# Two moves in a written-out schedule of a two-block transformer kernel: the order in which VectorE and TensorE handle the state outputs, and where ScalarE takes the squares of the final norm

## What is computed

```python
def ssd_chunked(x, dt, A, Bm, Cm):          # run forward and on the flipped sequence
    ...
    y_diag = jnp.einsum('bcgrls,bcsgrp->bclgrp', Wd, xdt)
    decay_states = jnp.exp(a_cs[..., -1:] - a_cs)
    states = jnp.einsum('bcsgn,bcgrs,bcsgrp->bcgrpn', Bc, decay_states, xdt)
    ...
    _, prev = lax.scan(step, init, (jnp.moveaxis(states, 1, 0), jnp.moveaxis(chunk_decay, 1, 0)))
    prev = jnp.moveaxis(prev, 0, 1)
    y_off = jnp.einsum('bclgn,bcgrpn,bcgrl->bclgrp', Cc, prev, jnp.exp(a_cs))
    return (y_diag + y_off).reshape(b, l, H, P)

        x = x + jnp.square(jax.nn.relu(h @ w_up[i])) @ w_down[i]
    return rmsnorm(x, norm_final)            # x * rsqrt(mean(x*x) + EPS) * g
```

## Time and profile before

| | |
|---|---|
| median of 3 runs | 1835.4 us (1835.2 to 1836.85) |
| the profiled execution, its own time | 1837.07 us |
| its span, first to last instruction | 1835.2 us |
| TensorE clock granted in it | 0.999 |
| TensorE busy | 1792.7 us, 98% |
| VectorE busy | 1178.2 us, 64% |
| ScalarE busy | 847.1 us, 46% |
| GpSimd busy | 260.2 us, 14% |
| chain that ended last | PE 70%, DVE 21%, ACT 5%, issue 4% |

### The profile page before, as it was taken

The page is one execution under the profiler, slowest core; times in us unless marked ns, Lnnn a source line. Parts: engine busy times, 40 slices in busy tenths (PEclk is TensorE's granted clock), DMA queues, the critical chain, the costliest instruction groups (busy, mean ns, idle before and its releaser), DMA issues.

```text
span 1835.2 us, 24785 instructions
## 1 busy us (share of the span) xinstructions
PE 1792.7 (98%) x9602; PEld 1453.2 (79%) x9602; DVE 1178.2 (64%) x1912; ACT 847.1 (46%) x1623; POOL 260.2 (14%) x324
## 2 busy tenths in 40 slices
PE   7999999999999989999999999999999999999997
PEld 7767898888888877878878786767788998888886
DVE  6356544233345788897888955677556358685957
ACT  5255533222224565564655644554434445343434
POOL 0502000000000035254352540000020000000000
PEclk9999999999999999999999999999999999999999
DMA  7211343332322453353443444233544241404211
GB/s 242 81 58 45 98 127 99 108 92 92 92 92 74 150 141 128 117 146 103 151 137 116 138 149 154 88 104 116 138 149 137 68 153 58 161 23 161 76 73 46
DMA packets 128244, 205.69 MB, mean 112 GB/s; under 512 B 26480, under 2 KB 58416, under 8 KB 127488
## 3 DMA queue, kind: packets, MB, share of 16 engines
q1 hardware_dynamic: 118944, 166.83, 28.6%
q0 software_dynamic: 8464, 34.93, 5.5%
q10 hardware_dynamic: 720, 2.36, 0.3%
HBM read 191.37 MB, written 12.71 MB: 111 GB/s over the span
## 4 chain that ended last, share of the span: by engine, by line
PE 70%; DVE 21%; ACT 5%; issue 4%; DMA 0%; POOL 0%; DVEq 0%; ACTq 0%
PE m L2135 13%; PE m L2137 13%; PE m L2136 13%; PE m L2146 5%; PE m L2148 5%; PE m L2147 5%; DVE lo L1387 4%; PE s L2298 3%; DVE X L1791 3%; PE m L2270 2%; PE m L2272 1%; PE m L2271 1%; PE m L2243 1%; PE m L2244 1%; PE m L2245 1%
## 5 line engine op out<-in xcount | busy, mean ns | idle before, releaser
L2135 PE MATMUL m<-hH,hi 128*128 128x512 f32 (+1 forms) x1392 | 531.6, 382 | 2.9 <-DVE hL L1417 1.6
L2137 PE MATMUL m<-hH,lo 128*128 128x512 f32 (+1 forms) x1392 | 509.6, 366 | 0.0
L2136 PE MATMUL m<-hL,hi 128*128 128x512 f32 (+1 forms) x1392 | 509.2, 366 | 0.0
L1387 DVE TENSOR_TENSOR lo<-raw,hi 128x1024 fp32r<-128x1024 f32 x267 | 333.0, 1258 | 162.1 <-ACT hi L913 161.8
L913 ACT ACTIVATE hi<-raw 128x1024 fp32r<-128x1024 f32 x267 | 276.5, 1050 | 176.2 <-PE m L2137 41.8
L2135 PEld LDWEIGHTS m<-hH,hi 128*128 128x128 f32 x1392 | 263.3, 189 | 50.1 <-issue 5.4
L2137 PEld LDWEIGHTS m<-hH,lo 128*128 128x128 f32 x1392 | 263.1, 189 | 43.3
L2136 PEld LDWEIGHTS m<-hL,hi 128*128 128x128 f32 x1392 | 263.6, 189 | 40.0 <-issue 1.0
L2146 PE MATMUL m<-hi,hH 128*128 128x512 f32 (+1 forms) x320 | 134.8, 421 | 1.8 <-DVE lo L1387 1.8
L2148 PE MATMUL m<-hi,hL 128*128 128x512 f32 (+1 forms) x320 | 122.1, 381 | 0.0
L2147 PE MATMUL m<-lo,hH 128*128 128x512 f32 (+1 forms) x320 | 122.0, 381 | 0.0
(11 more groups left out here) (331 smaller groups left out, 3006.9 us busy)
## 6 DMA issues: line engine op xcount, KB each, us to landing
raw<-in_w_in_dram SPq DMA_DIRECT2D x72, 512.0 KB, 3.7
hn<-scr_cs_dram POOLq DMA_DIRECT2D x32, 512.0 KB, 4.2
raw<-in_w_up_dram SPq DMA_DIRECT2D x32, 512.0 KB, 4.9
wq<-in_w_down_dram SPq DMA_DIRECT2D x24, 512.0 KB, 8.4
raw<-in_w_gate_dram SPq DMA_DIRECT2D x44, 256.0 KB, 2.9
raw<-in_w_up_dram SPq DMA_DIRECT2D x44, 256.0 KB, 3.2
raw<-in_w_down_dram SPq DMA_DIRECT2D x22, 512.0 KB, 4.0
raw<-in_w_in_dram SPq DMA_DIRECT2D x33, 256.0 KB, 3.3
```

What stands on the lines that cost most here:

```text
L1387: e.tensor_tensor(d, r, h.bitcast(F32), ALU.subtract).then_inc(s_lo, 1)
L2135: e.matmul(bank, wh[:, kk, c], h[:, k, q], start=k == 0, stop=False)
L2136: e.matmul(bank, wh[:, kk, c], l[:, k, q], start=False, stop=False)
L2137: x = e.matmul(bank, wl[:, kk, c], h[:, k, q], start=False, stop=k == kt - 1)
```

## The change

There are three edits. The third to sixth outputs of the first group of each round go one slot later (slots 33 to 36 become 34 to 37). The squares of results 2, 3, 8 and 9 in `fs3` come at the end of the slot behind the one in which they stood, behind `round_hidden` and `split_weights`. The root's preparation goes from slot 3 of `fs3` to slot 19.

```diff
-ROOT_AT = (s0("wo0") + 2, s0("dn20") + 2, s0("wa0") + 1, s0("fs3") + 3)
+ROOT_AT = (s0("wo0") + 2, s0("dn20") + 2, s0("wa0") + 1, s0("fs3") + 19)
...
-OF_T = [x + s + k for x in X0 for s in (31, 49) for k in range(6)]
+OF_T = [x + s for x in X0 for s in (31, 32, 34, 35, 36, 37, 49, 50, 51, 52, 53, 54)]
...
                 for b, i in DONE_AT.get(g, ()):
-                    final_squares(b, i)
+                    if i >= 10:
+                        final_squares(b, i)
                 round_hidden(g)
                 for j in CONV_AT.get(g, ()):
                     split_weights(j)
+
+                for b, i in DONE_AT.get(g - 1, ()):
+                    if i < 10:
+                        final_squares(b, i)
```

## The result

The changed kernel took 1840.18 us (median of 14 runs, 1838.39 to 1842.75); the kernel before, run between them on the same chip, took 1836.06 us (14 runs, 1835.12 to 1837.25). The ratio is 1.0022, with a 95% interval of 1.0015 to 1.0029: 0.22% slower, where the forecast said no difference, and 2.2 us above the upper end of its range. The runs of a kernel fall in two groups some 1.6 us apart (before: seven of 1835.12 to 1835.45 and seven of 1836.67 to 1837.25), and one execution of the kernel before in a later set, 3822.78 us, enters no comparison. Three of the 14 runs of the changed kernel are in its lower group (1838.39 to 1838.61), so the medians are 4.1 us apart and the lower groups 3.4.

The account below looks back on a forecast made before the run. TensorE, busy 1792.7 of 1835.2 us, was taken as the bound, leaving 42 us idle and the ends. Outputs +2.45 and `fs3` -2.2 gave +0.25 us on the 1835.4 median: 1835.6 us, range 1831.5 to 1838.0.

Parts of the forecast that it names:

- part 1: Outputs one slot later: the wait moves from the third output to the sixth and grows, +2.45 us over four rounds.
- a second wait: Rival: the sixth read-out comes late, so TensorE also waits at the second state matmul, +3.9 us; chance 0.06.
- a smaller gain in `fs3`: Rival: the second square, ahead of `hi5`, is met later; 0 to -1.1 us in place of -2.2; chance 0.08.
- The wait at the third output goes, and one ahead of the sixth takes its place: Rounds 1 to 3: the 1.41 us wait goes; TensorE idles 2 to 2.5 us before the sixth output.
- the head's multiply-adds: VectorE's L1791, now ahead of the fourth read-out, starts at 814.8 and takes 2.3 us, near the 2.69 us row.
- From its end to the fourth read-out: VectorE, from the end of the head's multiply-adds to the fourth read-out: 2.4 us of the same instructions.
- The first state matmul is 1.0 us later, and x+47 gives 0.3 back: Rounds 1 and 2: 0.95 us late at x+39, less 0.3 of old idle time at x+47's narrow matmul: +0.65 each.
- Round 0: First state matmul waits for the fifth read-out, second comes 1.4 us later; the wait at 721.70 gives some back: +0.8 us.
- No second wait for the sixth read-out: Sixth read-out ends by 824.1, before TensorE reaches the second state matmul at about 824.7, so no wait there.
- `fs3`, -2.2 us: Last stage: squares moved behind splits remove the waits for `fL` and the last weight split; result 9's add 2.2 us earlier.

Follow-up runs that it names:

- e3: The changed kernel with the third output back in its old slot, only the fourth to sixth a slot later; 1836.48 us, ratio 1.0001 to the kernel before.
- e5: e2 with the root's preparation back in slot 3 of fs3; 1834.78 us, ratio 0.999 to the kernel before.
- e2: The changed kernel's squares and root edits, with the outputs as in the kernel before; 1833.4 us, ratio 0.9986 to the kernel before.
- e4: The changed kernel with ten useless matmuls added ahead of the sixth output in rounds 1 to 3; 1837.24 us, ratio 1.0005 to the kernel before.
- e8: e2 with the first group of outputs in slots 30, 31, 32, 34, 34 and 36; 1836.56 us, ratio 0.9998 to the kernel before.
- e7: The changed kernel with the sixth output of the first group one more slot later (38); 1842.56 us, ratio 1.0037 to the kernel before.

## Why the prediction was wrong

**What failed.** The step is the sum of part 1, in which the moved wait is priced by its length alone (TensorE stands until 819.95, first state matmul 1.0 us later). The prediction foresaw 2 to 2.5 us of idle TensorE and did not ask what speed TensorE has behind it. Measured: behind the waits of rounds 2 and 3 the clock was 0.57 and 0.68 as a mean over four microseconds, and the way from the output to the state matmul took 1.4 and 1.6 us more than in round 1, which kept its clock. By the traces the kernel is 3.3 us slower, by the lower groups 3.4, so the miss is about 3.1 us, and the two falls make 3.0 of it. The medians give 4.1 and a miss of 4.12 - 0.25 = 3.9 us; the 0.7 us between is the mix of the two groups. Each kernel taken against the kernel before of its own set, the changed one has 4.1 - 0.7 = 3.4 us more than the one with filled waits and 4.1 - 0.0 = 4.1 us more than the one with the wait in two, each with an interval of about 1.5 us either way. This was in no rival either: the slower rivals were a second wait and a smaller gain in `fs3`.

The Trainium skill, TensorE: Matmul & The Clock Gate, section "HAM oscillation — how this bites in real kernels", tells of a kernel whose TensorE waits for its loads between groups of matmuls, falls to half rate, and starts the next group at it. The trace agrees with that in kind: 0.57 and 0.68 behind the wait, 0.43 us between matmuls for 0.23. The waits of the page's example are longer than these, so it names the mechanism and would not have said that 2.7 us is too much. I had not weighed this page, and gave the mechanism no chance.

**What held.**

- *The wait at the third output goes, and one ahead of the sixth takes its place.* Right. Its length was 2.68 us, forecast 2 to 2.5. The term that was off most is the head's multiply-adds, taken at 2.3 us:

```profile
813.80 2.52 DVE L1796 SCALAR_TENSOR_TENSOR X<-CBU,DT,X 128x128 f32<-128x128 f32 x4
...
818.70 0.41 DVE L1774 TENSOR_TENSOR OT<-s,ECS 128x256 f32<-128x256 f32 x1
```

  From its end to the fourth read-out are 818.70 - 816.32 = 2.4 us, as forecast.
- *The first state matmul is 1.0 us later, and x+47 gives 0.3 back.* Nearly: counted from the matmuls ahead of the group, the first state matmul of round 1 was 1.2 us later, and the second state matmul and x+47 gave some 0.3 and 0.35 back. Round 1, whose clock stayed whole, so came out at +0.5 us (forecast +0.65). In `e3` rounds 1 to 3 cost 0.6, 0.6 and 0.4 (forecast 0.65, 0.65, 0.35).
- *Round 0.* The wait is where it was forecast, and cost +0.8 us, as forecast:

```profile
706.33 0.70 PE L2480 MATMUL s<-XW,BTK 128*128 128x256 f32 x2 [2.21 <-DVE OT L1774]
```

- *No second wait for the sixth read-out.* Right: the second state matmul of round 1, at 823.74, has no idle time before it.
- *`fs3`, -2.2 us.* Right. ScalarE's rows beside the earlier trace rows, and VectorE's beside the earlier trace rows:

```profile
1801.04 1.06 ACT L902 ACTIVATE hi<-hn 128x1024 fp32r<-128x1024 f32 x1 [5.93 <-DVE hn L1577]
1802.01 0.61 ACT L853 ACTIVATE junk<-X 128x512 bf16<-128x512 f32 x1
...
1802.95 1.05 ACT L1049 ACTIVATE fH<-fa 128x1024 fp32r<-128x1024 f32 x1
```

```profile
1799.80 1.22 DVE L1577 TENSOR_TENSOR hn<-wq,hn 128x1024 f32<-128x1024 f32 x1
...
1818.74 1.21 DVE L1386 TENSOR_TENSOR lo<-wq,hi 128x1024 fp32r<-128x1024 f32 x1
1819.88 1.28 DVE L1510 TENSOR_TENSOR X<-m,X 128x512 f32<-128x512 f32 x2
```

  The weight split is first, then one square, then `fH`. The last split has no idle time before it, and the pair of adds comes 1819.88 - 1799.80 = 20.08 us behind the sum of weights, where it was 1818.41 - 1796.12 = 22.29: 2.2 us less. Medians give -2.1 (`e5`) and -3.1 us (`e2`), each with an interval of about 1.5 us either way; the lower groups give -2.0 for both.

## What to carry to other kernels

A wait of TensorE isn't priced by its length alone: when a change makes one longer, read the granted clock behind the waits that the kernel has, and give a rival to the case that it falls behind the new one. Here single waits of 1.4 us left the clock whole in every trace, and waits of 2.7 us cost up to 1.6 us more. The length alone is no safe measure: waits of about 2 us lost the clock in three traces (`e4`, `e5`, `e8`) and kept it in others. Where another engine's list sets the time, a new order only moves the wait, so spread it, and look for a gain where an instruction comes off the chain, as the squares did.

## What was not expected of the hardware

- The clock falls behind some waits and not behind others of the same length: in four traces never behind round 1's 2.7 us and always behind those of rounds 2 and 3, and in `e7` not behind 3.06 us. Nor does it fall at a fixed distance from the wait: in round 2 it is whole up to 934.1 and 0.50 from 934.14 us on in the first profile of the changed kernel, 0.3 us behind the start of the output (933.86), and in the second it is 0.50 from 934.88 on, 0.3 us ahead of it (935.15), with TensorE still waiting. Over the 14 runs of the changed kernel its mean was 0.997 in ten (1838.39 to 1840.65 us) and 0.994 to 0.996 in four (1840.09 to 1842.75 us), so some runs lose it more often than the profiled one. What decides it was not tested. The Trainium skill, TensorE: Matmul & The Clock Gate, section "What's actually happening", says that the gate's bookkeeping runs free of the program. The two distances from the output agree with that; that it decides which waits are hit is not shown by a run.
- Matmuls that compute nothing can be worth their place: five in each of three waits did as much as ten.
- The multiply-adds took 2.52 us where GpSimd worked beside them for 815.38 - 813.80 = 1.6 us, and 2.69 us where it worked beside them for 817.63 - 815.34 = 2.3 us (the prediction took 2.4, which is GpSimd's whole stretch); another head took 1.44 us. So 0.7 us less of overlap gave back only 0.17 us. GpSimd's rows there:

```profile
813.06 1.07 POOL L2037 TENSOR_TENSOR X<-hn,CS 128x512 f32<-128x512 f32 x1
...
814.77 0.61 POOL L2028 TENSOR_TENSOR XW<-XS,WST 128x256 f32<-128x256 f32 x1
```
